# First channel tile of the head taken token tile by token tile, and head loads in another order

## What is computed

```python
def rmsnorm(x, g):
    xf = x.astype(jnp.float32)
    y = xf * lax.rsqrt(jnp.mean(xf * xf, axis=-1, keepdims=True) + EPS)
    return (y * g.astype(jnp.float32)).astype(x.dtype)

def ada_modulation(cond, w_ada, b_ada):
    m = jax.nn.silu(cond) @ w_ada + b_ada
    return [t[:, None, :] for t in jnp.split(m, 6, axis=-1)]

def modulate(x, g, shift, scale):
    return rmsnorm(x, g) * (1 + scale) + shift

# of a layer
sh1, sc1, g1, sh2, sc2, g2 = ada_modulation(c, w_ada[l], b_ada[l])
h = modulate(xs, norm1[l], sh1, sc1)
a_b, a_c, a_u, q, k, v, cq, ckv, k_rope, f_u = split_projection(h @ lw['w_in'])
```

## Time and profile before

| | |
|---|---|
| three runs | 1187.94, 1188.1 and 2394.26 us; median 1188.1 |
| the profiled execution | 1190.82 us, of which the span of instructions is 1189.2 |
| PE busy | 1121.5 us, 94% of the span |
| DVE, ACT, POOL busy | 536.3, 282.8, 208.8 us |
| mean granted clock of PE | 0.992 |
| the chain that ended last | PE 84%, DVE 6%, DMA 4% |

### The profile page before, as it was taken

The page is one execution under the profiler, slowest core; times in us unless marked ns, Lnnn a source line. Parts: engine busy times, 40 slices in busy tenths (PEclk is TensorE's granted clock), DMA queues, the critical chain, the costliest instruction groups (busy, mean ns, idle before and its releaser), DMA issues.

```text
span 1189.2 us, 13631 instructions
## 1 busy us (share of the span) xinstructions
PE 1121.5 (94%) x4356; PEld 604.3 (51%) x4356; DVE 536.3 (45%) x1275; ACT 282.8 (24%) x653; POOL 208.8 (18%) x288
## 2 busy tenths in 40 slices
PE   5999999998999999999799999989899879999995
PEld 3556766554444454444355676745544435444442
DVE  1146543874237433433441545477623644333326
ACT  2121222663011211111141112156601111111111
POOL 5026101010115100000463410000112230000022
PEclk9999999999999999999999999999999999999998
DMA  9577822893207899998865941178300589999954
GB/s 350 209 245 289 315 109 92 349 370 145 107 26 279 323 386 366 368 367 302 322 231 154 388 149 36 43 293 337 107 18 0 189 343 354 359 373 371 358 176 196
DMA packets 63318, 291.17 MB, mean 245 GB/s; under 512 B 9504, under 2 KB 10672, under 8 KB 47328
## 3 DMA queue, kind: packets, MB, share of 16 engines
q1 hardware_dynamic: 33344, 190.87, 42.8%
q0 software_dynamic: 22720, 78.75, 18.6%
q10 hardware_dynamic: 7200, 20.87, 4.4%
HBM read 240.06 MB, written 56.98 MB: 250 GB/s over the span
## 4 chain that ended last, share of the span: by engine, by line
PE 84%; DVE 6%; DMA 4%; issue 2%; ACT 2%; POOL 1%; SPq 0%; ACTq 0%; POOLq 0%; DVEq 0%
PE ps L1235 13%; PE ps L1536 12%; PE ps L1715 9%; PE ps L1693 9%; PE ps L1696 9%; PE ps L1170 3%; PE ps L1163 3%; PE ps L1470 2%; PE ps L1501 2%; PE ps L1481 2%; PE ps L1146 2%; PE ps L1749 2%; DMA expert_in<-arena,pos_i 2%; PE ps L1145 2%; PE ps L1101 2%
## 5 line engine op out<-in xcount | busy, mean ns | idle before, releaser
L1235 PE MATMUL ps<-arena 128*128 128x320 f32 x560 | 156.6, 432 | 0.0
L1536 PE MATMUL ps<-arena 128*128 128x512 f32 x320 | 140.4, 594 | 2.4 <-issue 2.4
L1235 PEld LDWEIGHTS ps<-arena 128*128 128x128 f32 x560 | 105.0, 190 | 42.6 <-issue 1.0
L1715 PE MATMUL ps<-arena 128*128 128x512 f32 x256 | 115.4, 594 | 3.7 <-issue 3.7
L1693 PE MATMUL ps<-arena 128*128 128x512 f32 x256 | 117.2, 601 | 1.3 <-DVE arena L2791 1.3
L1696 PE MATMUL ps<-arena 128*128 128x512 f32 x256 | 115.1, 592 | 0.0
L2791 DVE COPY arena<-ps 128x512 f32<-128x512 f32 x32 | 22.1, 691 | 203.3 <-PE ps L1676 203.3
L1536 PEld LDWEIGHTS ps<-arena 128*128 128x128 f32 x320 | 59.5, 190 | 74.6 <-issue 74.6
L1693 PEld LDWEIGHTS ps<-arena 128*128 128x128 f32 x256 | 48.9, 192 | 62.5 <-issue 60.4
L1696 PEld LDWEIGHTS ps<-arena 128*128 128x128 f32 x256 | 48.6, 190 | 61.2 <-issue 61.2
L1715 PEld LDWEIGHTS ps<-arena 128*128 128x128 f32 x256 | 46.1, 190 | 50.5 <-issue 50.5
(11 more groups left out here) (332 smaller groups left out, 1652.2 us busy)
## 6 DMA issues: line engine op xcount, KB each, us to landing
arena<-in_w SPq DMA_DIRECT2D x96, 1024.0 KB, 9.3
arena<-in_w_ada SPq DMA_DIRECT2D x40, 1024.0 KB, 6.8
expert_in<-arena POOLq DMA_DIRECT2D x2, 8192.0 KB, 33.4
expert_out<-arena ACTq DMA_DIRECT2D x30, 512.0 KB, 8.1
arena<-expert_in POOLq DMA_DIRECT2D x28, 512.0 KB, 9.7
arena<-in_w_t SPq DMA_DIRECT2D x10, 1024.0 KB, 10.6
arena<-in_w_ada_c SPq DMA_DIRECT2D x8, 1024.0 KB, 13.2
arena<-in_w_out SPq DMA_DIRECT2D x8, 1024.0 KB, 6.1
```

The source lines that it names most:

```text
L1235: ins = mm(out[:, 0:HALF], lhs[:, k, :], rhs[:, k, :], start=(first and k == 0), stop=(last and k == 3), skip_group_check=True)
L1536: ins = mm(out[:, n * 512:(n + 1) * 512], yT[:, k, t * P:(t + 1) * P], w[k // 2][:, k % 2, n * 512:(n + 1) * 512], start=(k == 0), stop=(k ...
L1715: ins = mm(out[:, n * 512:(n + 1) * 512], hidT[:, f, :], w[:, f, n * 512:(n + 1) * 512], start=(f == 0), stop=(f == 1))
```

## The change

SP's list gets `wN0` ahead of token tiles 1 and 2. For channel tile 0 the transposes, ACT's copies and the narrow matmuls are done one token tile at a time: ACT copies 128 columns three times where it copied 384 once, and it does so between the squares of the token tiles. DVE makes channel tile 0's modulation between the rows of token tile 0 and 1. On PE narrow(0,0) comes ahead of modulation(1), and from then on modulation(k+1) and turn(k+1) come in period k instead of modulation(k+2) and turn(k+2), with sums(k+1) behind narrow(k,1). The numbers that `made` gives are those of the new order. `head_hT` now counts ten copies instead of eight.

```diff
@@ SP
             tokens_in(0)
             head_columns_in(0)
+            narrow_in(0, 0)
             tokens_in(1)
             tokens_in(2)
-            narrow_in(0, 0)
@@ PE
-                def head_turn(k):
-
-                    if k:
-                        pe.wait_ge(head_hT, k)
-                    for t in range(HEAD_TILES):
+                def head_turn(k, tiles):
+
+                    for t in tiles:
@@
                     head_modulation(0)
+                    pe.wait_ge(head_rows, 1)
+                    head_turn(0, [0])
+                    head_sums(0)
+                    chunk_wait(pe, 0, ("wN", 0))
+                    pe.wait_ge(head_hT, 1)
+                    head_narrow(0, 0)
+                    pe.wait_ge(head_rows, 2)
+                    head_turn(0, [1])
+                    pe.wait_ge(head_hT, 2)
+                    head_narrow(0, 1)
+                    head_modulation(1)
                     pe.wait_ge(head_rows, HEAD_TILES)
-                    head_turn(0)
-                    head_sums(0)
-                    head_modulation(1)
-                    head_turn(1)
-                    for k in range(KD - 1):
+                    head_turn(0, [2])
+                    pe.wait_ge(head_hT, 3)
+                    head_narrow(0, 2)
+                    head_turn(1, range(HEAD_TILES))
+                    head_sums(1)
+                    for k in range(1, KD - 1):
                         if k % 2 == 0:
                             chunk_wait(pe, 0, ("wN", k // 2))
-                        pe.wait_ge(head_hT, k + 1)
+                        pe.wait_ge(head_hT, HEAD_TILES + k)
                         head_narrow(k, 0)
+                        head_modulation(k + 1)
+                        head_turn(k + 1, range(HEAD_TILES))
+                        head_narrow(k, 1)
                         head_sums(k + 1)
-                        head_narrow(k, 1)
-                        if 0 < k < KD - 2:
-                            head_modulation(k + 2)
-                            head_turn(k + 2)
                         head_narrow(k, 2)
-                        if k == 0:
-                            head_modulation(2)
-                            head_turn(2)
@@ ACT
-            for t in range(HEAD_TILES):
-                first_square(t)
+            first_square(0)
+            first_square(1)
+            head_columns_out(0, made("tokens", 0), 0, 1)
+            first_square(2)
+            head_columns_out(0, made("sums", 0) + 1, 1, 2)
+            head_columns_out(0, made("product", 1) + 1, 2, 3)
@@ DVE
-                    for t in range(HEAD_TILES):
-                        head_row(t + 1, t)
-                    for k in range(KD):
+                    head_row(1, 0)
+                    head_move(0)
+                    head_columns_of(0)
+                    head_row(2, 1)
+                    head_row(3, 2)
+                    for k in range(1, KD):
                         head_move(k)
                         head_columns_of(k)
```

More of the change, by code:

```diff
@@ L636, in made @@
         def made(what, k):
-            return 3 * k + {"product": 1, "tokens": 2, "sums": 3}[what]
+            if k == 0:
+                return {"product": 1, "tokens": 2, "sums": 3}[what]
+            return 3 * k + {"product": HEAD_TILES, "tokens": HEAD_TILES + 1, "sums": HEAD_TILES + 2}[what] - (k == 1 and what == "product")
         head_ada = ps[:, 6 * BANK:6 * BANK + 2 * P]
@@ L1896, in _ @@
                             first_square(4)
-                    act.wait_ge(head_hT, KD)
+                    act.wait_ge(head_hT, HEAD_TILES + KD - 1)
                     act.sem_inc(head_copied, 1)
@@ L2250, in _ @@
                         head_row(t + 1, t)
-                    dve.wait_ge(head_hT, KD)
+                    dve.wait_ge(head_hT, HEAD_TILES + KD - 1)
                     dve.sem_inc(head_copied, 1)
```

10 lines of the change are left out of this document (5 added, 5 removed).

## The result

Over 20 runs of each kernel the median went from 1187.72 us to 1191.08: the ratio is 1.0027, with a 95% interval of 1.0014 to 1.0040. The change makes the kernel slower by 0.27%, about 3.2 us, far inside the 2% to which the chances were tied, but beyond the measurement's uncertainty. The medians are of all 20 runs; the ratio leaves out one run of each kernel, of 2394.26 and 1350.08 us, as slow executions. The prediction was 1190.3 with a range of 1187.3 to 1193.1, from a median of 1188.1. The profiled execution took 1192.96 us, its span is 1191.3, 2.1 us longer than in the earlier trace rows.

What follows compares the result with a forecast made beforehand. PE, busy 94% of a 1189.2 us span, was taken as the bound. +0.7 us in the head and +1.5 at product4(0) gave +2.2 on the median 1188.1: 1190.3, range 1187.3 to 1193.1.

Steps and rivals of the forecast that it cites:

- Both terms: +0.7 us in the head from PE's lower clock and +1.5 us of PE waiting at product4(0).
- signs that I had named for being wrong: narrow(1,0) before 24.5 or after 27.5, or PE still in steady periods; the clock's rise was to fall between 18 and 21.
- The front: First tile on PE: narrow(0,0) begins at 13.8 instead of 19.05, after ACT's square of tile 1 and its copy.
- The gaps: New PE waits in the head: 0.8 us after each single transpose, 1.45 after channel tile 1's sums, together 3.1.
- The clock: PE's rise from 1.2 to 2.4 GHz at 18.0 to 20.1 us, head 0.2 to 1.2 slower; at 22 or later, 2.2.
- The term of +0.7: Head: the middle taken between 0.2 and 1.2 us slower, as PE's earlier work runs at the lower clock.
- The steady periods: PE's periods after the head stay 6.6 us; one narrow pair of 1.56 to 1.66 covers the 1.45 reaction; cost 0.
- Rival E: Slower by over 2%: PE stops each steady period and the clock stays low, +46 us, 1234; chance 0.01.
- The queue behind the sums: sums(6), 1.56 us later, delays ACT's squares, POOL's list and DVE's third sum; PE waits 1.5 at product4(0), bounds 0 to 2.8.
- Rival B: POOL's mask additions catch up, so product4(0) does not wait; only the head's +0.2 to +1.2, 1188.3 to 1189.3; chance 0.27.
- Rival C: Faster as meant: shorter reactions or the clock rising at once with the work at 13.8; 1187.1 or 1186.4; chance 0.13.
- D: Slower by more, within 2%: clock late (+2.2) and bias transfers late (+2.8), +5 us, 1193.1; chance 0.09.

Runs made afterwards that it cites:

- the run with the old loads: The changed kernel with token tiles 1 and 2 loaded ahead of the first narrow weights again; ratio to the kernel before 1.0016.
- squares early: The changed kernel with the squares of token tiles 3 and 4 behind ACT's copy-out of channel tile 5 instead of 6; ratio to the kernel before 1.0016.
- later loads held back: The changed kernel with SP's first two w_t chunks and the Fourier tables held back until narrow(7,1) is done; ratio to the kernel before 1.006.
- the kernel with the most transposes: Channel tile 0 by token tiles, loads as before, product two channel tiles ahead, throwaway PE transposes (14, 10, 8, 3, 3); ratio to the kernel before 0.9948.
- with PE kept active: The changed kernel with throwaway identity transposes on PE: 14 at the start, then 6, 5, 2 and 2 in its gaps; ratio to the kernel before 0.9995.
- the kernel with 38 transposes: The kernel before with throwaway identity transposes on PE, 14 ahead of the first modulation and 24 behind it; ratio to the kernel before 0.9986.

## Why the prediction was right

The sum was +2.2 us, and 3.2 were measured. Both terms exist and the sign is that of the forecast; both were taken too small. Two of the signs that I had named for being wrong did show: in the first profile narrow(1,0) is at 28.09, behind the limit of 27.5 (25.61 in the second), and in neither profile did the clock rise between 18 and 21 us. So that the time came out so well is in part luck.

*The front.* First narrow pair at 13.8: measured 14.08 and 14.01. The number is good, but one step behind it was wrong: "DVE's bias inputs arrive at 9.61, so row 0 is ready as before". They arrived at 10.71. ACT's square, which I named as the gate, started at 11.84 and was over before the modulation was ready at 13.38 (13.11 + 0.27; the first is the start of DVE's last operation on it). So the 13.8 came out by luck: my chain to the modulation was 1.1 us short, and a wait that is not there filled the gap. I had costed the load moved forward for what it delays on its own queue, not for POOL's small transfers beside it. The run with the old loads shows that this is worth 1 us.

*The gaps.* 0.55 each instead of 0.8, since the reactions were shorter than I took them: 0.04 us from the end of the transpose to ACT's copy and 0.05 from its end to the pair, where I had 0.1 and 0.2. And 1.27 instead of 1.45: behind ACT's copy of three tiles PE also started after 0.05 us, not after the 0.24 that I added for the weight load.

*The clock.* I gave a rise between 18.0 and 20.1 us, with 22 or later as the bad case. Profiles of the same start gave 17.2 and 17.1 as well as 23.3 twice, and the head was 0.3 or 3.1 us slower for it. The term of +0.7 lies between and the mechanism is right: work at the lower level takes the earlier start back. But a rise is no number that can be had from one profile. The four profiles of exactly this head (the changed kernel twice, squares early, later loads held back) have narrow(1,0) at 26.7 on average, the two of the kernel before at 25.2: that would make the term 1.5, with a spread that four profiles can't narrow. And "5.1 us of idle PE to be had, and no more" left the clock out, since the kernel with the most transposes gained 6.2. The Trainium skill (TensorE: Matmul & The Clock Gate, "What you observe") gives half a microsecond as the spread between runs. The two profiles of the changed kernel differ by 6 us, and the measurement decides.

*The steady periods.* No profile shows PE stopping in them, and their length stays 6.6 us: ACT's copy-outs of two channel tiles in a row start at 53.63 and 60.23 in the changed kernel's timeline. Rival E did not occur: 1.27 of reaction and the weight load fit under one narrow pair.

*The queue behind the sums.* ACT's copy-out of channel tile 6 starts at 60.23 instead of 55.48 (the row is below). Less the 3.19 us by which PE's narrow(7,1) and all behind it is late, that is 1.56, the predicted number. Then the step that failed in size: I took 1.5 us for the wait, little more than the 1.35 of the sums alone, and 2.4 were measured, inside the bounds of 0 and 2.8. What I had as a bound came about in part: POOL waited 1.2 us longer for the bias transfers (18.06 against 16.84), since SP's loads, issued 3.1 us later against PE's work, lay more on top of them; held back altogether, they left it at 14.7. Three profiles with this order (the changed kernel twice, and with PE kept active) have the wait at 2.37 to 2.40, whatever the clock did; the one with the old loads, with sums and squares in the same place, has 0.86.

These are rows of the changed kernel's ACT, of the kernel before's POOL (the four loads, from which the 16.84 comes), and of the changed kernel's DVE:

```profile
60.23 0.67 ACT L1839 ACTIVATE arena<-ps,arena 128x384 f32<-128x384 f32 x1 [5.93 <-DVE arena L2246]
```

```profile
77.94 2.10 POOL L934 DMA_DIRECT2D arena<-bias_rows  x4 [14.72 <-issue]
```

```profile
95.61 2.18 DVE L2325 TENSOR_TENSOR arena<-arena 128x512 f32<-128x512 f32 x1
```

*Rival B* fell. The mask additions took 9.62 us, not less than 9.26, although DVE's first three weight sums beside them had shrunk to 0.68, 0.69 and 2.18 (the fourth, the row above, had grown from 0.69). Something of B did show with the old loads, where the additions took 8.77. Rival C, faster as meant, and D did not occur in the medians, though in the first profile the change was 5.75 us behind at product4(0), which is D's size.

## What to carry to other kernels

When a step is moved back within one engine's list, follow everything that stands behind it on the engines that it feeds: here sums moved by 1.56 us carried the squares, POOL's roots, its transfers and additions, and the price was paid 60 us later at a wait that had 0.2 us of slack. Where work starts earlier but with more gaps, ask what it does to the clock before counting the earlier start as won. When a change has several parts, measure them one by one: here the good part was hidden behind two that cost more. And where PE sits idle ahead of its first data, some tens of throwaway transposes can be worth more than a finer order of the first tile (3.5 us against 1.9), though they do not raise the clock in every execution.

## What the runs showed of the hardware that was not expected

PE's clock can be up before any data is there and fall again within a few us of work: in the kernel with 38 transposes it was at the upper level at 14.17 us and fell near 16.3, behind idle times of 1.67 and 0.59 us. With the same 14 transposes at the start it was up at 7.5 us in one profile, and not before 16.9 in another.

Spells of the lower level, most of them worth 1.5 to 2 us, came behind the head in every profile, one to five of them each time. Most lie near 384, 596, 784, 860, 944 and 972 us, single ones near 124, 208 and 404; all lie in or behind stretches in which PE waits. They go with the spread of the runs of one kernel, though how much of it they are is not shown: of the eight runs of the fastest version the two with a mean granted clock of 0.989 took 1190.2 and 1190.8 us, the other six, at 0.991 to 0.994, 1184.8 to 1187.4.

A load of 928 KB put ahead on SP's queue made the transfers of 3 to 8 KB on POOL's queue land later: they took 5.8, 5.8 and 6.4 us from issue to landing instead of 5.2, 5.1 and 5.3. DVE's operation that waits for the last of them starts at 10.46 to 10.71 us in each of the profiles that have this load first, against 9.50 to 9.81 in the others.

POOL's four mask additions took 8.4 to 10.2 us in layer 0; undisturbed they would take 7.2, four times the 1.81 of the earlier trace rows. DVE's overlap alone does not set this, as the changed kernel shows; what else does stays open.
